# Reordering TensorE's small score matmuls in the attention and recurrence groups of an encoder layer

## The reference

```python
xn = rmsnorm(x, norm_pre_w)
h = xn @ w_in                                  # 2048 x 13312
na_q, na_k, na_v, na_z, hg_q, hg_ff, hg_fb, hg_i, hg_z, gate_pre = split(h)
# branch a: 16 heads of 64; each query sees all 4 grid rows, 16 columns around its own
p = softmax(where(window, q @ k.T * 64**-0.5 + rel_bias, -inf)); o_a = (p @ v) * silu(na_z)
# branch b: 8 heads of 128, gated linear recurrence, forward plus backward:
#   S_t = diag(f_t) S_{t-1} + key_t (x) i_t,   o_t = S_t.T q_t,   f = lb + (1-lb) sigmoid(.)
o_b = rmsnorm(scan_fwd + scan_bwd) * silu(hg_z)
y = sigmoid(gate_a) * (o_a @ w_branch[:1024]) + sigmoid(gate_b) * (o_b @ w_branch[1024:])
out = x + rmsnorm(y @ w_out, norm_post_w)
```

## Time and profile before

| | us |
|---|---|
| median of 3 runs | 840.54 (840.07 to 840.79) |
| profiled execution, its own time | 840.67 |
| span of the profiled execution, first to last instruction | 838.9 |
| PE busy | 826.4 (99%) |
| PEld busy | 708.3 (84%) |
| DVE busy | 631.9 (75%) |
| ACT busy | 414.0 (49%) |
| DMA queue of the weights, share of 16 engines | 63.0% |

### The profile page before, as it was taken

The page is one execution under the profiler, slowest core; times in us unless marked ns, Lnnn a source line. Parts: engine busy times, 40 slices in busy tenths (PEclk is TensorE's granted clock), DMA queues, the critical chain, the costliest instruction groups (busy, mean ns, idle before and its releaser), DMA issues.

```text
span 838.9 us, 14167 instructions
## 1 busy us (share of the span) xinstructions
PE 826.4 (99%) x5006; PEld 708.3 (84%) x5006; DVE 631.9 (75%) x1053; ACT 414.0 (49%) x706; POOL 40.8 (5%) x48
## 2 busy tenths in 40 slices
PE   8999999999999999999999999999999999999996
PEld 7888788888888888888888888888888888888884
DVE  4767658788888888888888897897785778775443
ACT  6644445445445445445445445435545545544442
POOL 5000100000000000000100000100000000000002
PEclk9999999999999999999999999999999999999998
DMA  9755877666566566566567667656557767676522
GB/s 330 273 186 175 209 190 177 174 183 167 161 193 167 158 192 171 154 187 172 160 180 172 167 172 182 166 165 183 152 158 195 215 186 199 185 267 212 185 106 100
DMA packets 246708, 153.63 MB, mean 183 GB/s; under 512 B 15288, under 2 KB 228368, under 8 KB 246288
## 3 DMA queue, kind: packets, MB, share of 16 engines
q1 hardware_dynamic: 245664, 149.17, 63.0%
q10 hardware_dynamic: 1008, 3.98, 1.2%
HBM read 151.04 MB, written 2.10 MB: 183 GB/s over the span
## 4 chain that ended last, share of the span: by engine, by line
PE 91%; DVE 5%; ACT 2%; DMA 1%; issue 1%; POOL 0%; SPq 0%; POOLq 0%; ACTq 0%; DVEq 0%
PE psum L1173 47%; PE psum L1175 23%; PE psum L1414 3%; PE psum L1416 3%; PE psum L1415 3%; DVE w_lo L710 3%; PE psum L1276 2%; PE psum L1226 1%; PE psum L1228 1%; PE psum L1227 1%; ACT w_hi L447 1%; PE psum L1266 1%; DMA raw<-in_w_in 1%; PE psum L1242 1%; PE psum L1311 1%; PE psum L1255 1%
## 5 line engine op out<-in xcount | busy, mean ns | idle before, releaser
L1173 PE MATMUL psum<-act_hl,w_hi 128*128 128x512 f32 x1408 | 502.6, 401 | 0.0
L1175 PE MATMUL psum<-act_hl,w_lo 128*128 128x256 f32 x1408 | 394.9, 280 | 0.0
L710 DVE TENSOR_TENSOR w_lo<-raw,w_hi 128x1024 fp32r<-128x1024 f32 x272 | 325.1, 1233 | 82.5 <-ACT w_hi L447 82.3
L1173 PEld LDWEIGHTS psum<-act_hl,w_hi 128*128 128x128 f32 x1408 | 264.4, 188 | 64.8
L447 ACT ACTIVATE w_hi<-raw 128x1024 fp32r<-128x1024 f32 x272 | 273.6, 1053 | 40.2 <-PE psum L1416 25.6
L1175 PEld LDWEIGHTS psum<-act_hl,w_lo 128*128 128x128 f32 x1408 | 266.0, 189 | 0.0
L461 ACT ACTIVATE part<-psum 128x256 f32<-128x256 f32 x88 | 33.7, 383 | 218.2 <-PE psum L1175 218.1
L1173 PE MATMUL psum<-branch_hl,w_hi 128*128 128x512 f32 x256 | 90.6, 399 | 0.0
L1175 PE MATMUL psum<-branch_hl,w_lo 128*128 128x256 f32 x256 | 71.9, 281 | 0.0
L1173 PEld LDWEIGHTS psum<-branch_hl,w_hi 128*128 128x128 f32 x256 | 48.1, 188 | 12.0
L1226 PE MATMUL psum<-w_hi,branch_hl 128*128 128x512 f32 x128 | 50.4, 393 | 1.5 <-DVE w_lo L710 0.9
(11 more groups left out here) (137 smaller groups left out, 691.1 us busy)
## 6 DMA issues: line engine op xcount, KB each, us to landing
raw<-in_w_in SPq DMA_DIRECT2D x103, 1024.0 KB, 5.7
raw<-in_w_branch SPq DMA_DIRECT2D x16, 1024.0 KB, 6.0
raw<-in_w_out SPq DMA_DIRECT2D x16, 1024.0 KB, 5.1
bias_t<-in_na_rel_bias SPq DMA_DIRECT2D x32, 96.0 KB, 5.9
big<-in_x SPq DMA_DIRECT2D x4, 512.0 KB, 8.5
big<-in_x ACTq DMA_DIRECT2D x2, 1024.0 KB, 6.7
out<-big SPq DMA_DIRECT2D x5, 256.0 KB, 2.7
raw<-in_w_in SPq DMA_DIRECT2D x2, 512.0 KB, 6.7
```

What stands on the lines that cost most here:

```text
L710: nc.vector.tensor_tensor(w_lo[:, i, :], raw[:, r, 1024 * h:1024 * (h + 1)], w_hi[:, i, :].bitcast(F32), ALU.subtract).then_inc(lo_ready, 1)
L1173: nc.tensor.matmul(sums[h][:, :], w_hi[:, i, w], operand[:, k, :], start=first, stop=False, skip_group_check=True)
L1175: ins = nc.tensor.matmul(sums[h][:, 0:T], w_lo[:, i, w], operand[:, k, 0:T], start=False, stop=last, skip_group_check=True)
```

## The change

Only TensorE's program changes. The late near levels of the group before move from step 1 (middle of slot 2) to step 2 (middle of slot 3), right in front of the far scores; and `between` now runs the current group's `attention` step first and the left-over step behind it. In slot 3 the order was far scores, both scores; it becomes both scores, late near levels, far scores, and slot 2 holds no small matmuls. In slot 6 `turn_prob(g, 0)` comes before `hgrn_sum(g - 1)`. In the tail, which calls `previous` alone, the near levels move from the middle of its tile 2 to that of its tile 3, in front of the far scores. No other step has work on both sides.

```diff
             def previous(g, s):
-                if s == 1:
+                if s == 2:
                     near_session(g - 1, LATE_LEVELS)
-                if s == 2:
                     far_scores(g - 1)
                 if s == 5:
                     hgrn_sum(g - 1)
...
                         else:
+                            attention(g, s - 1)
                             if not first:
                                 previous(g, s - 1)
-                            attention(g, s - 1)
```

## The result

The changed kernel takes 836.19 us (median of 5 runs, 836.13 to 836.39) against 840.6 of the kernel before beside it (840.07 to 841.28): 0.9946 of it, 95% interval 0.9933 to 0.9958. It is 4.4 us faster, about three times the 1.4 us that were forecast, and outside the range. The profiled execution took 836.39 around a span of 834.7.

A forecast was written before the change was run, and what follows sets the result against it. TensorE, busy 826.4 of 838.9 us and never waiting inside a group, was taken as the bound. Seven groups saving 0.20 each, 1.4 us, with 0 in the tail and slot 6, gave 839.1 us from 840.54; range 838.1 to 840.5.

The forecast's parts named there:

- the first part: Opening section on what bounds the kernel: inside a group TensorE never waits, so group time is what it issues.
- 0.354 us a pair: In the projections: one w_hi and one w_lo matmul take 0.354 us, read over 19 pairs, 231.93 to 238.65.
- The sum of the crossings: Slot 3's session of scores, near and far, array shape changes included, costs 2.62 us; a group pays 0.20 less.
- Rows to columns: Slot 3, from the scores' 64 by 128 array shape directly to near's 128 by 64: taken as 0.14 us, bounds 0 to 0.34.
- the cheap crossing: Rival, slot 3: going from the scores' array shape to near's costs nothing, saving 2.4 us, 838.1 us; chance 0.15.
- The tail's session: In the tail, near levels and far come together: 1.28 + 0.43 us before and after.
- part (2): Tail: near levels and far, until now alone in slots 2 and 3, come together; change in time 0.
- Slot 6's order: Slot 6: turn_prob now precedes hgrn_sum, both 128 by 128, so no array shape change is altered: 0 on TensorE.
- The wait on qk_lo: Slot 3's scores wait for qk_lo, which in the closest group ends 1.0 us before TensorE arrives: costs nothing.
- VectorE's read of the scores: Scale-and-bias of the scores (L743), needing scores and late near levels: starts at about 246.75, 0.65 us earlier.
- if the span falls by other than the sum over the seven groups: Sign that the prediction is wrong: the whole span's fall differs from the groups' summed savings, forecast 7 x 0.20 = 1.4 us.
- Less than 0.1 behind the last scores pair's due time: Sign that the prediction is wrong, slot 3: first near pair stands under 0.1 us behind the last scores pair's due time.

## Why the prediction was wrong

**The step that failed** is in the first part: "The projections are a steady stream of pairs", "0.354 us a pair". That rate was read in one slot of one group and used as a constant, so that "the time of a group is the sum of what PE issues" had only the sessions in it. The pairs have two rates 2% apart (0.347 and 0.354), they are 56.6 of the 63.4 us of a group, and which one holds is set at each session. Reordering a session therefore had a second price, for everything up to the next one, and none of the rivals held it. It was readable: in group 0 the kernel before runs 33 pairs at 0.347.

**What held.** The sum of the crossings: 2.62 forecast, 2.63 measured; alone, a group is 0.19 shorter (0.20 forecast). Rows to columns costs a gap of 0.09, so the cheap crossing is out, though its 838.1 was nearer to the time. The tail's session costs 1.72 against 1.71 forecast; what was wrong in part (2), "0", is what came behind it, +0.5 in the tail and -1.7 in the branch stage. Slot 6's order is worth 0. The wait on qk_lo had the forecast margin, and VectorE's read of the scores came at 246.83 (246.75 forecast), from the timeline of the kernel after:

```profile
246.83 0.69 DVE L743 SCALAR_TENSOR_TENSOR wide<-psum,bias_t 128x512 f32<-128x512 f32 x1 [1.06 <-PE psum L1276]
...
368.47 0.69 DVE L851 TENSOR_TENSOR branch_hl<-na,branch_hl 128x512 fp32r<-128x512 f32 x1
...
370.25 0.98 PE L1242 MATMUL psum<-branch_hl 64*128 64x256 f32 x12
```

qk_lo ends 1.09 ahead of the scores in what was the closest group (1.0 forecast). Of its signs of being wrong, "if the span falls by other than the sum over the seven groups" is the one that came. "Less than 0.1 behind the last scores pair's due time" came too, by 0.01, and means nothing: that bound stood at the size of the gap itself.

**What stays open** is why a given session leaves PE at one rate or the other. The experiments show that the rate depends on the session, on what it meets (the same swap works behind one group and not behind another) and changes with PE's own stream alone; nothing outside PE was varied by itself. No rule was found that forecasts it.

## What to carry to other kernels

Before pricing a reorder of an engine that never waits, measure the rate of its steady work in every stretch, not in one: two levels in the same instructions mean that the reorder can move the level, for far more than the pieces moved. Then test the reorder together with variations that add no instruction (here the order inside the first pair behind a break), and read the time from one group to the next in the trace, which told 0.05 us where the medians scattered by 1. Here the array's shape changes added up as crossings, and merging sessions paid only when a crossing went.

## What the hardware showed that was not expected

In the kernels before and after, both with a mean granted clock of TensorE of 0.997 (1.00 in the branch stage), a w_hi (512 columns) and a w_lo (256) matmul of a full array take 0.353 or 0.347 us a pair, and stay at one for up to 16 projections. In the kernel after, the steps of the slow rate repeat every three pairs (w_hi to w_lo 0.241, 0.236, 0.233; w_lo to w_hi 0.120, 0.113, 0.117), those of the fast one every two (0.232, 0.231; 0.118, 0.112) or every one (0.230; 0.117). The output stage's matmuls of 512 columns follow each other by 0.227, which would make 0.340 a pair: 0.3400, 0.3467 and 0.3534 lie 0.0067 apart, and no run shows why.
